# RWKV-7 chunk inversion: from 64-column blocks to 32x32 diagonal blocks, with the last level as one block per half

## What is computed

```
def step(S, inp):
    r_t, w_t, k_t, v_t, kk_t, a_t = inp
    sa = einsum('bhij,bhj->bhi', S, kk_t)
    S = (S * w_t[:, :, None, :] - sa[..., None] * (kk_t * a_t)[:, :, None, :]
         + v_t[..., None] * k_t[:, :, None, :])
    return S, einsum('bhij,bhj->bhi', S, r_t)
```

## Time and profile before

| what | value |
|---|---|
| median of three runs | 2118.87 us (2115.19 to 2121.08) |
| the profiled execution | 2119.79 us, span 2117.8 us |
| busy: PE, DVE, ACT, POOL | 1980.8, 1304.2, 895.8, 769.2 us (94, 62, 42, 36%) |
| chain that ended last | PE 77%, DVE 11%, ACT 7%, issue 2%, others 1% or less |
| of it on L1537, the inversion's products | 5% |
| mean granted clock of TensorE | 0.975 |
| moved by DMA | 169.42 MB, mean 80 GB/s |

### The profile page before, as it was taken

The page is one execution under the profiler, slowest core; times in us unless marked ns, Lnnn a source line. Parts: engine busy times, 40 slices in busy tenths (PEclk is TensorE's granted clock), DMA queues, the critical chain, the costliest instruction groups (busy, mean ns, idle before and its releaser), DMA issues.

```text
span 2117.8 us, 47803 instructions
## 1 busy us (share of the span) xinstructions
PE 1980.8 (94%) x20520; PEld 1836.1 (87%) x20520; DVE 1304.2 (62%) x2049; ACT 895.8 (42%) x1701; POOL 769.2 (36%) x603
## 2 busy tenths in 40 slices
PE   6999999888999999999979999988889989999998
PEld 5998866677898999999979987657778989999998
DVE  5755347566679888831239452675566898888112
ACT  4535554333445444531154364544343544445221
POOL 5332244333433434332213321742252334343431
PEclk8999999899999999999989999999999999999999
DMA  8553210000122332344225432000001222232221
GB/s 271 162 169 120 78 19 2 22 28 3 47 77 60 94 86 80 88 140 140 83 90 180 149 109 61 9 22 3 28 25 51 70 77 84 80 91 78 75 80 67
DMA packets 255272, 169.42 MB, mean 80 GB/s; under 512 B 23873, under 2 KB 228223, under 8 KB 255063
## 3 DMA queue, kind: packets, MB, share of 16 engines
q1 hardware_dynamic: 254835, 166.32, 26.1%
q10 hardware_dynamic: 227, 0.07, 0.0%
HBM read 162.21 MB, written 4.15 MB: 79 GB/s over the span
## 4 chain that ended last, share of the span: by engine, by line
PE 77%; DVE 11%; ACT 7%; issue 2%; SPq 1%; POOL 1%; DMA 1%; DVEq 0%; ACTq 0%; POOLq 0%
PE PS L1126 12%; PE PS L1128 12%; PE PS L1127 12%; PE PS L1809 7%; PE PS L1810 7%; PE PS L1811 7%; PE PS L1537 5%; PE PS L1084 2%; ACT arena L2177 1%; SPq L542 1%; PE PS L1559 1%; DVE U_r L3195 1%; DVE U L2806 1%; ACT whi_r L2006 1%; PE PS L1192 1%
## 5 line engine op out<-in xcount | busy, mean ns | idle before, releaser
L781 POOL TENSOR_TENSOR ring_r<-ring,whi_r 128x1024 fp32r<-128x1024 f32 (+1 forms) x128 | 311.3, 2433 | 685.4 <-ACT whi_r L2006 685.4
L1126 PE MATMUL PS<-rwp_r,whi_r 128*128 128x320 f32 x1440 | 455.7, 316 | 12.4 <-DVE arena_r L2468 4.6
L1128 PE MATMUL PS<-rwp_r,ring_r 128*128 128x320 f32 x1440 | 448.0, 311 | 0.0
L1127 PE MATMUL PS<-U_r,whi_r 128*128 128x320 f32 (+1 forms) x1048 | 323.9, 309 | 0.0
L1126 PEld LDWEIGHTS PS<-rwp_r,whi_r 128*128 128x128 f32 x1440 | 273.3, 190 | 26.5 <-issue 19.5
L1127 PE MATMUL PS<-arena_r,whi_r 128*128 128x320 f32 (+1 forms) x904 | 282.3, 312 | 0.0
L1128 PEld LDWEIGHTS PS<-rwp_r,ring_r 128*128 128x128 f32 x1440 | 273.2, 190 | 0.0
L2006 ACT ACTIVATE whi_r<-ring 128x1024 fp32r<-128x1024 f32 (+1 forms) x128 | 131.2, 1027 | 296.1 <-PE PS L1128 295.2
L1127 PEld LDWEIGHTS PS<-U_r,whi_r 128*128 128x128 f32 x1048 | 196.9, 188 | 0.3
L2464 DVE TENSOR_TENSOR arena<-arena 128x640 f32<-128x640 f32 x32 | 61.2, 1912 | 214.8 <-ACT arena L1945 214.4
L1127 PEld LDWEIGHTS PS<-arena_r,whi_r 128*128 128x128 f32 x904 | 172.8, 191 | 0.2
(11 more groups left out here) (506 smaller groups left out, 4956.1 us busy)
## 6 DMA issues: line engine op xcount, KB each, us to landing
ring<-in_ffn_w SPq DMA_DIRECT2D x120, 512.0 KB, 3.8
rwp<-in_ada_w SPq DMA_DIRECT2D x64, 512.0 KB, 4.8
ring<-in_w_in SPq DMA_DIRECT2D x50, 512.0 KB, 4.6
U<-in_ada_w SPq DMA_DIRECT2D x16, 512.0 KB, 9.2
ring<-in_w_out SPq DMA_DIRECT2D x16, 512.0 KB, 3.8
arena<-in_ada_w SPq DMA_DIRECT2D x16, 512.0 KB, 4.6
ring<-in_ffn_w SPq DMA_DIRECT2D x16, 384.0 KB, 3.2
out<-arena SPq DMA_DIRECT2D x5, 512.0 KB, 3.6
```

Source lines behind the costliest of these rows:

```text
L781: g.tensor_tensor(rings_r[:, slot_of[n], 0:size(n), :], slot(n)[:, 0:size(n), :], whis[:, q % 2, 0:size(n), :].bitcast(F32), ALU.subtract) ...
L1126: mm(out, w[0][:, k, :], hi[:, cols], start=start, stop=False)
L1127: mm(out, w[0][:, k, :], lo[:, cols], start=False, stop=False)
L1128: return mm(out, w[1][:, k, :], hi[:, cols], start=False, stop=stop)
```

## The change

All small matrices of the inversion are kept for 32x32 diagonal blocks: a partition holds only the 32 columns of its own block (`M16D`, `MLD`, `ID32`, `QQ` of 2x4x32, new `X32`, `PL0`, `PL1` of 4x32), so DVE and ACT handle 128 columns a matrix instead of 256, and `each` makes four products of 32x32x32 a head instead of two of 64x64x64. The diagonal products are made for 32x32 blocks (32 a direction instead of 16, `QT` masked straight from PSUM, no `PT`). `PL0`'s source is computed again later, next to L1577, with the one 32x32 block of each half that lies off the diagonal (`PL1`; 24 more products a direction, banks 4d and 4d+1, columns 384 on); DVE masks the first and negates the second. The last level works on that block alone (`crossing`: 8 products each for PL1 X, for the transpose of X and for the last product, `INTO` and `FROM` naming the blocks), its result is copied into the full `X` by DVE in two instructions a direction, and POOL (`diagonals`) copies the diagonal blocks of `X32` into `X` in four, in place of the level masks; `solved(0)` waits for it (`pl_ready`). The two wide products L1559 and L1577 stay; L1577 moves ahead of round 2. `prep_scan` and `decays` of the next chunk are split: direction 0 where both stood (on ACT one step later, behind the copies of the 16-level), direction 1 behind the copies of the last-level operands on ACT and behind `adds(3, 5)` on DVE. The scalings and `y_low` on DVE stand behind the last `adds`. In chunk 4 ACT's first weight split stays ahead of the last-level copy and the second goes behind it. On POOL the next chunk's keys, and in chunk 4 the gates, stand behind `diagonals`. A chunk has 1,024 small PE instructions instead of 512.

```diff
 # TensorE
-for n in range(4):
-    q, t_ = n % 2, (n // 2 + n) % 2
-    mm(PS[half[t_], a + 2 + q, 64 * f:64 * f + 64], b["KB"][half[q], f, 1, half[t_]],
-       rk[half[q], f, wk, half[t_]], start=True, stop=True)
+for p in BLK:
+    for q in range(2):
+        mm(PS[p, a + 2 + q, 32 * f:32 * f + 32], kb[half[q], f, p], rk[half[q], f, wk, p],
+           start=True, stop=True)
...
 def each(d, bank, col0, lhs, rhs):
     for hh in range(RWKV_H):
-        for t_ in half:
-            ins = mm(PS[t_, 4 * d + bank, col0 + 64 * hh:col0 + 64 * hh + 64], b[lhs][t_, hh, :], ...)
+        for p in BLK:
+            ins = mm(PS[p, 4 * d + bank, col0 + 32 * hh:col0 + 32 * hh + 32], b[lhs][p, hh, :], ...)
+def crossing(d, bank, col0, lhs, rhs, source):
+    for hh in range(RWKV_H):
+        for h in range(2):
+            to, p = BLK[INTO[d][h]], BLK[source[d][h]]
+            ins = mm(PS[to, 4 * d + bank, col0 + 32 * hh:col0 + 32 * hh + 32], b[lhs][p, hh, :], ...)
...
-for l in range(2):
-    for d in range(2):
-        added(d, 2 + l)
-        each(d, 2, 0, "PL%d" % l, "X")
-        each(d, 2, 256, "X", None).then_inc(s["inv_mm"], 1)
-    for d in range(2):
-        copied(d, 3 + l)
-        each(d, 3, 0, "QT", "Q").then_inc(s["inv_mm"], 1)
+for d in range(2):
+    added(d, 2)
+    pe.wait_ge(s["rw_pt"], at["rw_pt"] + 2 * k + d + 1)
+    each(d, 2, QQ0, "PL0", "X32")
+    each(d, 2, QQ0 + P, "X32", None).then_inc(s["inv_mm"], 1)
+for d in range(2):
+    copied(d, 3)
+    each(d, 3, X0, "QT", "Q").then_inc(s["inv_mm"], 1)
+for d in range(2):
+    added(d, 3)
+    crossing(d, 2, X0, "PL1", "X32", FROM)
+    crossing(d, 3, X0, "X32", None, INTO).then_inc(s["inv_mm"], 1)
+for d in range(2):
+    copied(d, 4)
+    crossing(d, 3, X0, "QT", "Q", INTO).then_inc(s["inv_mm"], 1)
...
 # ScalarE
-        if k < NC - 1:
-            decays(k + 1)
-        for l in range(2):
-            copies(3 + l, 4 + 2 * l)
+        copies(2, 2, slice(1, 2))
+        copies(3, 4)
+        if k < NC - 1:
+            decays(k + 1, 0)
+        copies(4, 6)
+        if k < NC - 1:
+            decays(k + 1, 1)
...
 # VectorE
+            masked("Q", a + 2, 0, M16D[d]).then_inc(s["dve_step"], 1)
+            masked("QT", a + 2, 64, M16D[1 - d]).then_inc(s["rw_q"], 1)
...
+        adds(2, 3)
 (RBT, both directions)
+        adds(3, 5)
+        if k < NC - 1:
+            prep_scan(k + 1, (1,))
+        adds(4, 7)
+        if k == 2:
+            ssd_scaled(range(2))
+        if k == 4:
+            for n in range(4):
+                y_low(n)
...
 # GpSimd
+def diagonals(k):
+    for d in range(2):
+        pool.wait_ge(s["inv_add"], at["inv_add"] + 10 * k + 7 + d)
+        for n, p in enumerate(BLK):
+            ins = g.tensor_copy(b["X"][p, :, 32 * (n % 2):32 * (n % 2) + 32], b["X32"][p])
+        ins.then_inc(s["pl_ready"], 1)
+    pool.wait_ge(s["pl_ready"], at["pl_ready"] + 2 * k + 2)
```

More of the change, by code:

```diff
@@ L288, in build @@
             b["BR"] = take(1024).rearrange("p (h w t) -> p h w t", h=4, w=2)
-            b["QQ"] = take(512).rearrange("p (w h t) -> p w h t", w=2, h=4)
+            b["QQ"] = take(256).rearrange("p (w h t) -> p w h t", w=2, h=4)
             b["Q"], b["QT"] = b["QQ"][:, 0], b["QQ"][:, 1]
-            for n in ("PT", "PL0", "PL1", "X", "CR", "RHS"):
+            for n in ("X32", "PL0", "PL1"):
+                b[n] = take(128).rearrange("p (h t) -> p h t", h=4)
+            for n in ("X", "CR", "RHS"):
                 b[n] = take(256).rearrange("p (h t) -> p h t", h=4)
@@ L730, in compact @@
                 def compact(dst, src):
-                    for half in range(2):
-                        q = slice(64 * half, 64 * half + 64)
-                        g.tensor_copy(dst[q, :], src[q, 64 * half:64 * half + 64]).then_inc(setup["pool"], 1)
+                    for p in BLK:
+                        g.tensor_copy(dst[p, :], src[p, p]).then_inc(setup["pool"], 1)
                         pool.wait_ge(setup["pool"], step())
@@ L739, in _ @@
                 blocks(full[1], 32)
-                blocks(full[2], 64)
                 blocks(BO[:, :], 64)
[L742 to L747, removed]
+                compact(ID32, ident[:, :])
+                g.tensor_tensor(full[3], full[1], full[0], ALU.subtract).then_inc(setup["pool"], 1)
+                pool.wait_ge(setup["pool"], step())
                 for d, sg in ((0, 1), (1, -1)):
@@ L752, in _ @@
                     sel(full[4], [[sg, P]], -sg, 0, ALU.is_gt)
[L753 to L756, removed]
+                    for dst, own in ((M16D[d], full[0]), (MLD[d], full[3])):
+                        g.tensor_tensor(full[5], full[4], own, ALU.mult).then_inc(setup["pool"], 1)
+                        pool.wait_ge(setup["pool"], step())
+                        compact(dst, full[5])
                     for w, op in ((d, ALU.is_gt), (1 - d, ALU.is_ge)):
@@ L2904, in adds @@
                                     dve.wait_ge(s["rw_x"], at["rw_x"] + 2 * k + d + 1)
-                                v.tensor_tensor(b["X"], b["X"], heads(PS[:, 4 * d + 3, 0:256], 4), ALU.add).then_inc(
-                                    s["inv_add"], 1)
+                                x = heads(PS[:, 4 * d + 3, 384:512], 4)
+                                if n < 4:
+                                    v.tensor_tensor(b["X32"], b["X32"], x, ALU.add).then_inc(s["inv_add"], 1)
+                                    continue
+                                for j in INTO[d]:
+                                    ins = v.tensor_copy(b["X"][BLK[j], :, 32 * (1 - j % 2):32 * (1 - j % 2) + 32],
+                                                        x[BLK[j]])
+                                ins.then_inc(s["inv_add"], 1)
                         for d in range(2):
```

176 lines of the change are left out of this document (95 added, 81 removed).

## The result

The changed kernel takes 2220.98 us (median of four runs, 2216.47 to 2221.73), the kernel before 2118.59: a ratio of 1.0485, 95% interval 1.0469 to 1.0501. The forecast was 2078 us, the range 2060 to 2102. The change costs 102 us where 41 were to be gained.

A forecast was written before the change was run, and what follows sets the result against it. It took the chain through the inversion to bound each of ten chunks. Savings of 25.2 us a layer, 50 in all, less 9 for the clock, gave 41: from 2118.9 to 2078 us, range 2060 to 2102.

The forecast's parts named there:

- Price of a product: Inversion's small PE products: 32x32 on four tiles cost 7.5 ns an instruction, 0.24 us a group instead of 0.47.
- The issue allows it: Within the product price: PE can start two instructions for different tiles about 10 ns apart or less.
- D: Rival, 0.03: PE's issue binds; each ns above 7.5 between small products costs 0.9 us a chunk; 2244 us.
- Front of the chunk: First mask to the next group of products: 4.4 us falls to 1.7, saving 2.7 a chunk.
- Inner part: Inversion from L1559 to the state products before L1609: 18.1 us falls to 13.3, plus 0.3 for decays; saves 4.8.
- chain of latencies: Inversion after round two: ACT copies, product groups and DVE adds in series, from 6.9 to 13.3 us after L1559.
- C, a small tile is no quicker: Rival, 0.10: a tile stays taken 58 ns however small the product; saving only 11, 2108 us.
- The clock: PE's granted clock in chunks 1 to 4: one low stretch in each of eight at 1.7 us; 9 us lost.
- B: Rival, 0.20: the clock stays low, three or four low stretches a chunk through front and inner part; saving 21, 2098.
- Chunks that differ: Chunks not saving the plain 7.2 us: k=0 5.8, k=1 6.0, k=2 6.1, k=3 4.8, k=4 2.5; 25.2 a layer.
- The term for chunk 4: Last chunk: moved DVE and POOL work keeps output projection at 28 us after L1559; only the front's 2.5 saved.

The follow-up runs named there:

- the dose of 8 columns: Kernel before, each of 224 inversion products a chunk preceded by the same product of 8 columns, 448 matmuls a chunk more; 2221.35 us, ratio 1.0467.
- the paired products: Changed kernel with products of two heads made one of 64 columns, 400 matmuls a chunk fewer, heads 1 and 3 wrong; 2121.49 us, ratio 1.0002.
- the run with 896 more matmuls: Kernel before with 32x32 products of all four heads added in front of each inversion group, 1,658 matmuls a chunk; 2304.26 us, ratio 1.0884.
- the stream of 64x64: Kernel before plus three streams without waits behind its last transposes: 32x32 on four tiles, 64x64 on four, 64x64 on two; 2368.09 us in all.
- the run with fewer products: Changed kernel without the second squares, 192 of 1,262 matmuls a chunk fewer, ACT copying half as much there, inverse wrong; 2167.17 us.
- the dose of 448: Kernel before with 32x32 products of two heads added in front of each inversion group, 1,210 matmuls a chunk; 2198.06 us, ratio 1.0373.

## Why the prediction was wrong

**The step that failed is in "Price of a product": "The issue allows it".** It took two instructions that start 10 ns apart or less and 16 that start 13 ns apart for the rate of a chunk. They were a rate only for instructions that are already there, and the 1,024 of the forecast left out the weight load that has to be brought in with each matmul. The price of 7.5 ns is about right inside a packet and at the full clock (94 matmuls at 425.29 take 1.00 us less a tail of some 0.2, 8.5 ns each; 16 more in a dose took 0.12 us, 7.5 each; at a clock of 0.50 a burst of 128 takes 1.93 us, 13 each), and wrong over a chunk, where the supply's 28 to 29 ns stands in its place. The nearest rival was **D**, which had issue as the bound and even a total near the measured one (2244). But it looked for the bound between two starts, argued it away with short rows, and got 0.03. That its total comes near is luck: its 27 ns were the price of narrow products on two tiles in turn, which the dose of 8 columns found again with PE busy, and only happen to be like the supply's 28.

The trace of before held what was needed. Its page has 162 packets for 41,040 instructions of PE, and this view of its instruction queue from 424.89 to 458.2 has six in a chunk, in a kernel where two tiles in turn need 29 ns a matmul anyway:

```profile
q8 instruction: 6, 0.10, 1.2%
```

In the changed kernel the window from 425 to 466 has

```profile
q8 instruction: 10, 0.16, 1.7%
```

Packets in the kernel before never come closer than 3.5 us. Ten of them in the 26 us that the forecast wanted for a chunk, one in 2.6 us, would have been a rate that no stretch of 2.1 ms showed. Such a view does not prove a limit, since this kernel seldom asks for more; it says that the forecast asked for something that nothing on record supported. The Trainium skill, "Runtime: NRT & Kernel Launch", section "Instruction fetch mechanics", describes the mechanism, blocks of 256 instructions fetched through a queue of PE's own, and calls the cost of crossing from one block to the next mostly hidden. The packets agree with the blocks; that the crossing is hidden holds in the kernel before and not in the changed one, where the gaps are 93.6 us.

**Front of the chunk.** Forecast 1.7 us from the first mask to the wide product; measured 424.74 to 428.42, 3.7, of which 1.70 is the gap for issue: 2.0 without it. In the kernel before, without the 32x32 products, the front part gave 10 us in ten chunks.

**Inner part.** Forecast about 13.8 to L1636, measured 25.0 (428.42 to 453.46). The timeline's gaps for issue in it sum to 7.7; with the paired products the stretch is 16.0 (416.96 to 432.96), and 2.1 of that are gaps for issue. So the forecast's chain of latencies was near, 2 us too short at the most, where the supply took 7 and more; the rest of the 25.0 lies at a low clock and was not taken apart.

**C, a small tile is no quicker**, was the wrong way round for 32x32 and right for a narrow product on a large tile: 8 columns cost what 64 do, 29 ns. The forecast put that down to the 64-column weights of its row; these runs agree and do not prove it.

**The clock.** B's fact came true and not its price: 0.75 and 0.79 over the chunks shown, far below the 0.95 counted on. It is not what opens the gaps: the run with 896 more matmuls had 57.9 us of them at 0.98, the stream of 64x64 40% of its time at 0.97, and the run with fewer products won 53.8 us at a hardly higher clock. It rose to 0.95 in chunk 1 of the paired kernel, which has fewer gaps and twice the columns in a product; which of the two raised it, and how much of the 102 us the low clock took beside the supply, is not settled.

**Chunks that differ.** The moved side work of chunks 2 and 3 was priced at 1.1 and 2.4 us a layer, 7 us in both; putting most of it back, and chunk 4's `y_low` with it, gave 9. The term for chunk 4 was wrong in more than the supply: it had the output projection 28 us after the wide product, as before (527.00 to 555.03), and a front 2.5 us shorter. The paired kernel has 35.9 and 38.0 us in the two layers, and 33.4 and 35.2 with `y_low` put back. There POOL's gates start 18.8 us after L1570 (533.03) where the forecast had 12.5, behind eight diagonal copies that take 4.7 us, and PE waits 2.4 and 3.8 us for them; gaps for issue ahead of them in that chunk are 1.7 us. PE's wait for DVE's right-hand side was there in the changed kernel already, 13.3 us in 6 places, beside the gaps for issue.

**The split.** Worth 16 us alone in the kernel before, with the one scaling moved along, where its wait of 1.44 us in eight chunks would be 12; in the changed kernel about 5, inside the noise.

## What to carry over

Before a product is cut into smaller ones, count the instructions of the stretch and divide by what the instruction queue has ever delivered in this trace: here 128 matmuls in some 3.6 us, with some two packets in hand at most. A matmul quicker than 28 ns wins only in short bursts between slower work. Spacing between neighbours shows what an engine can do with instructions that it has; the packets show how many it will have.

## What the runs showed of the hardware that was not expected

- In the streams instructions reach PE no faster than 28 to 30 ns a matmul with its weight load, 16 KB in 3.5 to 4.0 us, with no other traffic in the way, at a granted clock of 0.50 and of 0.97.
- After 35 us of easy work 330 instructions ran before PE stopped for more.
- A matmul of 8 columns on two 64x64 tiles in turn costs 29 ns on average, as one of 64 does; on four 64x64 tiles a burst of 128 takes 2.09 us, so 15 ns each.
- The stream of 32x32 stopped for 27.1 of 57.2 us and had a granted clock of 0.50 in a window of 20 us inside it, that of 64x64 for 23.7 of 58.8 us and had 0.97.
- A change of tile shape between 64x64 and 32x32 costs 0.14 us, worked out from the dose of 448.
